# Products of the identity with itself, placed ahead of the first transposes and the first projection on the matmul engine

## The reference, cut to what matters

```python
h = layer_norm(x, ln0_g, ln0_b)            # 304 rows x 1024
xa, ga, vb, gb, q, k, v, r, z = split(h @ w_in)
y = concat([rglru(conv(xa)) * gelu(ga),    # linear recurrence
            silu(layer_norm(conv31(vb * sigmoid(gb)))),
            gated_linear_attention(q, k, v, z) * silu(r)]) @ w_out
h = layer_norm(ALPHA * h + y)
out = layer_norm(ALPHA * h + moe(h))       # top 4 of 32 experts, 12 MB of weights each
```

## Time and profile before

| | us |
|---|---|
| median of three runs | 1119.19 |
| the profiled execution's own time | 1119.61 |
| its span, first to last instruction | 1117.9 |
| TensorE busy (products) | 1078.0 (96%) |
| VectorE busy | 349.6 (31%) |
| ScalarE busy | 160.1 (14%) |
| mean DMA rate over the span | 381 GB/s |

### The profile page before, as it was taken

One profiled execution on the slowest core, in us unless ns is written; L12 is line 12 of the kernel. 1 busy time (PEld: TensorE's weight loads), 2 busy tenths in 40 slices (PEclk: granted clock), 3 DMA queues, 4 the chain that ended last, 5 costly groups with the idle time before them and its releaser, 6 DMA issues.

```text
span 1117.9 us, 13864 instructions
## 1 busy us (share of the span) xinstructions
PE 1078.0 (96%) x5441; PEld 472.0 (42%) x5441; DVE 349.6 (31%) x829; ACT 160.1 (14%) x307; POOL 40.9 (4%) x101
## 2 busy tenths in 40 slices
PE   7999999999999999999999999999999999999996
PEld 4677547343434343434343333333333343434342
DVE  4797663313131313131313131212121213122124
ACT  4254604000100010001000100010101010101002
POOL 8000400000000000000000000000000000000000
PEclk9999997999999999999999999999999999999998
DMA  9533645999999999999999999999999999999992
GB/s 294 193 151 158 265 193 214 401 427 428 427 429 429 427 429 429 427 429 429 427 430 429 428 429 429 428 429 429 427 429 430 427 429 430 427 430 429 429 427 82
DMA packets 41094, 425.63 MB, mean 381 GB/s; under 512 B 6073, under 2 KB 12606, under 8 KB 16489
## 3 DMA queue, kind: packets, MB, share of 16 engines
q1 hardware_dynamic: 39185, 423.61, 90.5%
q0 software_dynamic: 1888, 1.75, 0.6%
HBM read 423.38 MB, written 2.17 MB: 381 GB/s over the span
## 4 chain that ended last, share of the span: by engine, by line
PE 73%; DMA 23%; DVE 2%; ACT 1%; issue 0%; SPq 0%; DVEq 0%
PE bank L1785 33%; DMA ring<-in_moe_w_dram 23%; PE bank L1800 10%; PE bank L1441 9%; PE bank L1742 7%; PE bank L1755 5%; PE bank L1698 2%; PE bank L1468 1%; PE bank L1810 1%; PE bank L1750 1%; PE bank L1446 1%; PE bank L1664 0%; PE bank L1688 0%; PE bank L1842 0%; DMA xt<-in_x_prompt_dram 0%; PE bank L1580 0%
## 5 line engine op out<-in xcount | busy, mean ns | idle before, releaser
L1785 PE MATMUL bank<-ring,hT 128*64 128x512 f32 x2048 | 454.9, 595 | 17.0 <-DMA ring<-in_moe_w_dram 16.8
L1785 PEld LDWEIGHTS bank<-ring,hT 128*64 128x64 f32 x2048 | 141.6, 137 | 302.3 <-issue 275.3
L1800 PE MATMUL bank<-ring 128*64 128x512 f32 x1024 | 226.8, 595 | 0.0
L1800 PEld LDWEIGHTS bank<-ring 128*64 128x64 f32 x1024 | 70.7, 137 | 132.6 <-issue 126.0
L1339 DVE TENSOR_SCALAR ring<-bank 128x512 f32<-128x512 f32 x32 | 22.1, 692 | 322.2 <-PE bank L1785 322.2
L1742 PEld LDWEIGHTS bank<-ring 128*128 128x128 f32 x792 | 93.3, 196 | 26.3 <-issue 26.0
L1742 PE MATMUL bank<-ring 128*128 128x128 f32 x792 | 99.7, 284 | 0.2 <-DVE ring L1286 0.2
L1356 DVE COPY ring<-bank 64x512 f32<-64x512 f32 x32 | 22.2, 694 | 230.1 <-PE bank L1800 230.1
L875 ACT ACTIVATE ring<-ring 128x512 f32<-128x512 f32 x32 | 20.1, 630 | 395.0 <-DVE ring L1339 395.0
L1292 DVE COPY hT<-bank 128x512 f32<-128x512 f32 x33 | 22.7, 688 | 140.3 <-PE bank L1742 140.3
L1755 PE MATMUL bank<-ring 128*128 128x512 f32 x128 | 63.5, 618 | 0.0
(11 more groups left out here) (300 smaller groups left out, 609.1 us busy)
## 6 DMA issues: line engine op xcount, KB each, us to landing
ring<-in_moe_w_dram SPq DMA_DIRECT2D x192, 2048.0 KB, 30.5
ring<-in_w_in_dram SPq DMA_DIRECT2D x5, 1536.0 KB, 13.3
ring<-in_w_out_dram SPq DMA_DIRECT2D x2, 2048.0 KB, 11.2
ring<-in_w_in_dram SPq DMA_DIRECT2D x1, 2048.0 KB, 13.3
lnbc<-in_ln_g_dram SPq DMA_DIRECT2D x3, 512.0 KB, 11.6
lnbc<-in_ln_b_dram SPq DMA_DIRECT2D x3, 512.0 KB, 11.4
xt<-in_x_prompt_dram SPq DMA_DIRECT2D x2, 512.0 KB, 3.9
ring<-in_state_gla_dram POOLq DMA_DIRECT2D x4, 144.0 KB, 5.3
```

Source lines behind the costliest of these rows:

```text
L1785: ins = pe.matmul(bank[b][64 * h:64 * h + 64, :], xT[:, q, k, j * CAP:(j + 1) * CAP], ring[:, c:c + 512], start=False, stop=k == KT - 1)
L1800: ins = pe.matmul(bank[OUT_BANK[j]][64 * h:64 * h + 64, :], actT[:, j, k % 4, (k // 4) * CAP:(k // 4 + 1) * CAP], ring[:, c:c + 512], star ...
```

## The change

Seventeen products `ident` x `ident` after the wait for the identity and ahead of the wait for the layer norm's rows; eight ahead of the transposes of tile 0; eight ahead of those of tile 1; five ahead of the waits for V0. No wait and no DMA is added, moved or removed.

```diff
+            def warm(n):
+
+                for _ in range(n):
+                    pe.matmul(bank[7][:, 0:P], ident[:, :], ident[:, :], start=True, stop=True)
+
             pe.wait_ge(consts_ready, 1)
+            warm(17)
             pe.wait_ge(ld_lncol, 32)
             job("LNC", lambda b: transposes([(b[:, 0:16], lnrow[0:16, :], 16)]))
...
+            warm(8)
             x_job("X0a", 0, 0, 4, P)
             x_job("X0b", 0, 4, 4, P)
+            warm(8)
             x_job("X1a", 1, 0, 4, P)
             x_job("X1b", 1, 4, 4, P)
+            warm(5)
             copied(pe, "X0a")
             copied(pe, "X0b")
             pe.wait_ge(ld_win["v"], 16)
```

## The result

The changed kernel takes 1121.68 us (median of 20 runs, 1119.97 to 1125.41), the kernel before 1118.99 us in as many runs (1115.43 to 1121.41). The ratio is 1.0031, with a 95% interval of 1.0023 to 1.0039: 3.5 us slower (2.6 to 4.4); the medians alone are 2.7 apart. The profiled execution took 1121.43 us, with a span of 1119.6. Forecast were 1123.7 us, range 1121.1 to 1126.2.

What follows compares the result with a forecast made beforehand. TensorE was taken to bound the start and set when the full DMA stream begins. New products, less faster transposes, make V0 4.5 us late: 1119.61 + 4.5 = 1124.1, as a median 1123.7 us, range 1121.1 to 1126.2.

Steps and rivals of the forecast that it cites:

- The bound and the path: TensorE's chain from the start sets when the full weight stream begins; V0 4.5 us late delays the end equally.
- Two records a product: At the start, each new identity product counts as two TensorE records: 38 products, 76 records.
- rival A: At the start, identity products cost one record each, so V0 keeps its time: 1119.3 us; chance 0.05.
- The price of a record: Each new record at the start costs 120 ns at full clock and 229 ns at half clock.
- The rise of the clock: TensorE's clock at the start rises 5.0 us after the first new product, at 7.87 us; ends 2.5 and 6.0.
- The cover beside TensorE: At the start, VectorE's and ScalarE's shifted work stays hidden behind V0, with cover 2.4 us deep.
- Rival B: After V0, a late engine or weight stream absorbs the shift and the time stays 1119.2 us; chance 0.04.
- the first `room` issue: First weight load needing a used slot, at 186.51 us before, should come 4.5 us later.
- Rival C: V0 ran at half clock throughout before; the change gives back 5.4 us there, reaching 1118.3 us; chance 0.02.
- Rival D: The mostly zero identity does not raise the clock; half clock lasts into V0, 1132 us or more; chance 0.03.
- The first layer's start: Start of `first_layer`, after the router, at 182.8 us before, should come 4.5 us later.
- The allowance for the low clock: For varying low clock around the router and gather, the range was widened 0.5 us below and 2.0 above.

Runs made afterwards that it cites:

- e1: Changed kernel with only the seventeen products, the other 21 removed; ratio 1.0003 to the kernel before.
- e3: Changed kernel with every count doubled to 34, 16, 16 and 10 products; median 1131.12 us, ratio 1.0116 to the kernel before.
- e5: Kernel before plus 6, 3, 2 and 1 products at the same four places, sized to fit the holes; median 1118.23 us, ratio 1.0002.
- e6: Kernel before, start unchanged, plus six identity products ahead of H1a, before the router; median 1117.23 us, ratio 0.9990.
- e8: Kernel before, start unchanged, plus six identity products ahead of H1a and six ahead of P2; median 1115.49 us, ratio 0.9974.
- e7: Kernel before, start unchanged, plus six identity products ahead of H1a and four ahead of the gather; median 1117.56 us, ratio 0.9994.
- e4: Kernel before with no new product, V0 waiting in addition for the next projection's weights; ratio 1.0072 to the kernel before.

## Why the prediction was right, and where it was off

- **The bound and the path: right.** A late V0 passes one for one. Five kernels have V0 later by 0.69, 3.50, 3.61, 7.5 (5.5, and 2.0 of V0 itself) and 12.16 us, and the ratios give 0.3, 3.5, 2.6, 8.1 and 13.0, each interval holding its own (V0's start is from one execution of each).
- **Two records a product: right.** 76 records for 38 products. So rival A is out.
- **The price of a record: 120 ns was taken, 112 is right.** The sixteen ahead of tile 1 take 1.79 us (11.39 to 13.18), 112 ns each. The gather's 120 was too dear and the transposes' 107 too cheap; with 16, 16 and 10 records this is 0.2 us of the sum.
- **The rise of the clock: the mis-sized term.** "A rise 5.0 us later, at 7.87" gave 9.33 us for the end of the seventeen; they were done at 8.47. With 229 and 112 ns a record, 5.59 us is 15 records at half clock and 19 at full: the rise came about 3.5 us after the first product, inside the ends kept (2.5 to 6.0). That is 0.86 of the 1.02 us by which V0 came earlier than forecast (15.17 against 16.19). In e1 the same start needed about 5.5 us. The halfway value was a single choice for something that varies by 2 us from one execution to the next.
- **The cover beside TensorE: right.** VectorE's and ScalarE's moved copies made nobody wait; X2 followed V0 without a hole. ScalarE's copy of X1a ended at 17.9 us (19.1 was worked out), V1 began at 21.05.
- **Rival B (absorbed) fell** with e3 and the table; the first `room` issue is at 189.09 instead of 186.51, 2.58 late in that pair, 3.50 less the mixer's 1.74 plus 0.82. The text had said that this shift would equal V0's but for the later low clock. It had looked for that only around the router; in the mixer it is as large.
- **Rival C (V0's clock) fell** as stated, with V0 at half clock throughout and 5.4 us to gain: the change is slower, and e5, with V0 at full clock and on time, is not faster beyond its interval. Its milder form, a late rise that costs V0 about 1 us, does occur (e6 and e8: 1.2 and 0.8 us). The argument against it rested on one execution.
- **Rival D fell:** identity products bring the clock up as others do.
- The first layer's start came out 2.58 late in the profile, less than 3.50 by the low stretches and the router part, as summed above. The medians' 2.7 lies within the ratio's interval; why it is nearer to its low end is not shown.
- **The allowance for the low clock was drawn too narrow.** It took the spread from three runs, 2.05 us; twenty lie 6 us apart. The median, 1121.68, still fell into the range, 0.6 us above its low end; V0's 1.02 us is half of its distance from the forecast.

## What to carry to other kernels

Filler on an engine that works in order has to be sized by the hole, in records and not in products, and at the clock that it will find: the same twelve records took 1.6 us in e6 and 2.9 in e7. What is over goes onto the path in full. First ask whether what follows the hole runs at low clock at all: here V0 did so in part in two of four executions, for about 1 us, and the best fill there shows no gain, while P2 and the router, where the granted clock is 0.50, gave 0.3% with six products each (e8). And ask who holds the engine once its clock is up (e6). And where single executions differ by several microseconds, compare marks (the start of a stage) and the low-clock time between them, not two spans.

## What the runs showed of the hardware that was not expected

- Low-clock stretches also come in the dense part. The mixer has TensorE busy throughout, yet 0, 3.4, 6.8 and 10.2 us of it ran at half clock in different executions. e1's two stretches, one to 97.2 and one from 104.1, with full clock between:

```profile
90.45:97.20 6.75, 6.75 (x26) 4.96 (x27) 5.36 (x13) 2.58 (x3) 0.00 (x0) 0.50 0.00 0
97.30:104.00 6.70, 6.70 (x63) 5.18 (x61) 2.46 (x4) 1.71 (x6) 1.54 (x7) 1.00 0.46 152
104.10:107.40 3.30, 3.30 (x15) 2.37 (x14) 2.51 (x7) 0.55 (x2) 0.00 (x0) 0.50 1.06 452
```

- The spread of the kernel before, 6 us in 20 runs, goes with it. Of the 23 runs beside e1 to e4, the three from 1115.5 to 1117.1 us have a mean granted clock of 0.990 or 0.991, the slowest, at 1121.7, has 0.984, and the others have 0.986 to 0.988. The part from `first_layer` to the end repeats within 0.12% in all traces (934.0 to 935.0 us).
- The clock column reads 1.00 at the start of a trace, before its first recorded change, when the durations show half clock: in e4 it is 1.00 for the stretch in which V0's first records run.

```profile
17.20:21.20 4.00, 4.00 (x7) 2.18 (x8) 0.00 (x0) 0.00 (x0) 4.00 (x9) 1.00 1.07 317
```

Seven records stand in those 4.0 us, the first and the last in part; at the changed kernel's 5.33 / 16 = 333 ns each there would be twelve.
